# Expert slots of a decoder step: token rows turned two slots ahead and written back in place

## What is computed

```python
combine = jnp.einsum('nk,nke->ne', w_top, jax.nn.one_hot(eid, N_EXPERTS, dtype=jnp.float32)).astype(h.dtype)
out = jnp.zeros_like(hf)
for e in range(N_EXPERTS):
    act = jax.nn.silu(hf @ P['moe_w_gate'][l, e]) * (hf @ P['moe_w_up'][l, e])
    out = out + combine[:, e:e + 1] * (act @ P['moe_w_down'][l, e])
```

## Time and profile before

| What | Value |
|---|---|
| Median of three runs | 2000.77 us |
| Lowest and highest run | 1998.65 and 2010.49 us |
| Span of the profiled execution, first to last instruction | 1993.9 us |
| TensorE busy | 1815.5 us, 91% |
| VectorE, ScalarE busy | 34%, 26% |
| Mean granted clock of TensorE | 0.970 |
| Expert stage of layer 0, first up product's end to last | about 787 to 1058 us |
| Expert stage of layer 1 | about 1672 to 1944 us |

### The profile page before, as it was taken

How to read it: one execution, slowest core, us unless ns; L and a number is a source line. 1 busy time by engine, 2 the same in 40 slices (tenths; PEclk the granted TensorE clock), 3 DMA queues, 4 the chain that set the end, 5 groups by cost and what they waited for, 6 DMA issues and landing times.

```text
span 1993.9 us, 52709 instructions
## 1 busy us (share of the span) xinstructions
PE 1815.5 (91%) x23279; PEld 1445.3 (72%) x23279; DVE 684.8 (34%) x1812; ACT 513.2 (26%) x1199; POOL 100.7 (5%) x155
## 2 busy tenths in 40 slices
PE   5999998999987898999998899999999989999983
PEld 3776777777776677888887754785666778888882
DVE  5241135666664332110113400416777240101105
ACT  2112223333332121111111201316777231111112
POOL 2112000000000001000001000000000001000002
PEclk9999999999999898999999999998999998999996
DMA  8665744433334497999999891642000387999964
GB/s 294 188 219 199 255 150 135 137 116 99 98 98 130 128 291 289 359 372 353 374 380 239 207 197 44 206 94 66 1 2 2 80 342 285 389 367 373 363 222 153
DMA packets 186742, 413.48 MB, mean 207 GB/s; under 512 B 53686, under 2 KB 123794, under 8 KB 178034
## 3 DMA queue, kind: packets, MB, share of 16 engines
q1 hardware_dynamic: 167746, 357.95, 54.7%
q0 software_dynamic: 11040, 39.85, 5.6%
q10 hardware_dynamic: 7760, 12.79, 1.8%
HBM read 356.84 MB, written 57.91 MB: 208 GB/s over the span
## 4 chain that ended last, share of the span: by engine, by line
PE 47%; issue 7%; ACT 3%; DVE 3%; DMA 2%; DVEq 0%; POOL 0%; ACTq 0%; SPq 0%
PE bank L1984 11%; PE bank L1979 6%; PE bank L1997 5%; PE bank L2003 3%; PE bank L1705 3%; PE bank L2816 3%; PE bank L2924 2%; PE bank L2872 2%; PE bank L2961 2%; ACT xsT L2166 2%; PE bank L1961 1%; PE bank L1972 1%; DMA rows<-y_slots,pos 1%; PE bank L2748 1%; PE bank L2893 1%
## 5 line engine op out<-in xcount | busy, mean ns | idle before, releaser
L1979 PE MATMUL bank<-wg,xsT 128*32 128x384 f32 x1056 | 121.9, 500 | 17.9 <-ACT xsT L2166 17.9
L1984 PE MATMUL bank<-wg,xsT 128*32 128x128 f32 x1056 | 123.2, 278 | 0.0
L1984 PE MATMUL bank<-wu,xsT 128*32 128x128 f32 x1056 | 119.2, 273 | 2.5 <-issue 2.5
L1979 PE MATMUL bank<-wu,xsT 128*32 128x384 f32 x1056 | 117.9, 486 | 3.3 <-issue 3.3
L1997 PE MATMUL bank<-wd,actT 128*32 128x384 f32 x1056 | 117.6, 486 | 1.6 <-ACT actT L2180 1.6
L1984 PEld LDWEIGHTS bank<-wu,xsT 128*32 128x32 f32 x1056 | 115.2, 110 | 5.2 <-issue 2.7
L2003 PE MATMUL bank<-wd,actT 128*32 128x256 f32 (+1 forms) x704 | 118.2, 326 | 0.0
L1984 PEld LDWEIGHTS bank<-wg,xsT 128*32 128x32 f32 x1056 | 116.0, 112 | 1.0
L640 PE MATMUL bank<-xm,wp 128*128 128x272 f32 x480 | 113.3, 395 | 0.0
L2376 DVE COPY ys<-bank 128x384 f32<-128x384 f32 x32 | 17.8, 558 | 265.4 <-PE bank L2003 265.4
L2368 DVE TENSOR_TENSOR act<-bank,act 128x384 f32<-128x384 f32 x32 | 17.9, 558 | 255.9 <-PE bank L1984 255.9
(11 more groups left out here) (632 smaller groups left out, 4022.9 us busy)
## 6 DMA issues: line engine op xcount, KB each, us to landing
wg<-in_moe_w_gate_dram SPq DMA_DIRECT2D x22, 2048.0 KB, 17.8
wu<-in_moe_w_up_dram SPq DMA_DIRECT2D x22, 2048.0 KB, 22.4
wd<-in_moe_w_down_dram SPq DMA_DIRECT2D x22, 2048.0 KB, 18.6
xT<-in_ada_w_dram SPq DMA_DIRECT2D x40, 1024.0 KB, 5.8
w<-in_moe_w_gate_dram SPq DMA_DIRECT2D x10, 2048.0 KB, 17.0
fT<-in_moe_w_up_dram SPq DMA_DIRECT2D x10, 2048.0 KB, 22.2
gall<-in_moe_w_down_dram SPq DMA_DIRECT2D x10, 2048.0 KB, 17.4
wp<-in_rwkv_w_rkv_dram SPq DMA_DIRECT2D x24, 512.0 KB, 4.6
```

The source lines that it names most:

```text
L1979: mm = pe.matmul(ps[32 * j:32 * j + 32, 0:GW], B.xsT[:, k, 32 * j:32 * j + 32], w[:, k, 0:GW], start=k == 0, stop=k == KT - 1)
L1984: mm = pe.matmul(ps[96:128, q * 128:(q + 1) * 128], B.xsT[:, kk, 32 * q:32 * q + 32], w[:, kk, GW:FF], start=kk == 0, stop=kk == KT - 1)
```

## The change

The tile `xsT` goes. The turned rows of a slot are written into the slot's own row buffer, `B.xs[j]`, over the rows they came from. TensorE turns the rows of slot s+2 behind the up product of slot s, where it turned those of s+1. In slot 0 it turns both slot 1 (in the old place) and slot 2 (between its gate and its down product); the last two slots turn nothing. VectorE's copy waits for both halves of the turn, since it writes over rows of either. SyncE loads token rows when the up product of the slot that used the buffer is done, where it waited for the turn. A filler tile `moe_spare` of the size of `xsT` stays in its place.

```diff
-    B.xs = [sb(st, f"xs{i}", [C, D]) for i in range(2)] + [B.hx[0:C]]
+    B.xs = [sb(st, f"xs{i}", [128, D]) for i in range(2)] + [B.hx]
+    B.xsT = [x[:, 0:KT * C].rearrange("p (k c) -> p k c", k=KT) for x in B.xs]
     B.hs = B.hx[0:NS]
     B.ys = [sb(st, f"ys{i}", [128, YW]) for i in range(3)]
-    B.xsT = sb(st, "xsT", [128, KT, C])
+    sb(st, "moe_spare", [128, KT * C])
...
         e = sp.value_load(B.slot_e[0:1, bass.ds(slot, 1)], min_val=0, max_val=E_N - 1)
-        sp.wait_ge(S("x_tr"), n * 2 + 2)
+        sp.wait_ge(S("up_mm"), n * 4 + 4)
         load_tokens(j, slot)
-        sp.wait_ge(S("up_mm"), n * 4 + 4)
         load_gate_up(sp, B, io, l, j, e)
...
-    def turn(j, n, h):
-
-        if h == 0:
-            pe.wait_ge(S(f"xs_loaded{j}"), (n if j else n - l - 1) * 16)
-        for k in range(4):
-            mm = pe.transpose(bank[6 + h][:, k * C:(k + 1) * C], B.xs[j][0:C, (4 * h + k) * 128:(4 * h + k + 1) * 128], B.ident[0:C, 0:C])
-        mm.then_inc(S("x_tr"), 1)
-
-    def gate_or_up(w, ps, done):
+    def turn(j, n):
+
+        pe.wait_ge(S(f"xs_loaded{j}"), (n if j else n - l - 1) * 16)
+        for h in range(2):
+            for k in range(4):
+                mm = pe.transpose(bank[6 + h][:, k * C:(k + 1) * C], B.xs[j][0:C, (4 * h + k) * 128:(4 * h + k + 1) * 128], B.ident[0:C, 0:C])
+            mm.then_inc(S("x_tr"), 1)
+
+    def gate_or_up(x, w, ps, done):
...
-                mm = pe.matmul(ps[32 * j:32 * j + 32, 0:GW], B.xsT[:, k, 32 * j:32 * j + 32], w[:, k, 0:GW], start=k == 0, stop=k == KT - 1)
+                mm = pe.matmul(ps[32 * j:32 * j + 32, 0:GW], x[:, k, 32 * j:32 * j + 32], w[:, k, 0:GW], start=k == 0, stop=k == KT - 1)
...
-    def slot(v, j, last):
+    def slot(v, j, left):
         n = prior_uses(regs, l, v, j)
         s = slot_count(regs, l, v, j)
-        v2, j2 = (v, (j + 1) % 3) if j else (0 if v is None else v + 1, 1)
-        gate_or_up(B.wu[j], bank[1], "up_mm")
-        if not last:
-            for h in range(2):
-                turn(j2, uses(regs, l, v2, j2), h)
+        v1, j1 = slot_after(v, j)
+        v2, j2 = slot_after(v1, j1)
+        gate_or_up(B.xsT[j], B.wu[j], bank[1], "up_mm")
+        if v is None:
+            turn(j1, uses(regs, l, v1, j1))
+        elif left > 1:
+            pe.wait_ge(S("xt_ev"), s * 2 + 4)
+            turn(j2, uses(regs, l, v2, j2))
         pe.wait_ge(S("act_ready"), s + 1)
         for c in range(3):
             mm = pe.transpose(bank[2 + c // 2][:, c % 2 * 128:c % 2 * 128 + 128], B.act[:, c, :], B.ident[:])
         mm.then_inc(S("at_mm"), 1)
-        if not last:
+        if left:
             pe.wait_ge(S("xt_ev"), s * 2 + 4)
             pe.wait_ge(S("silu_done"), s + 1)
-            pe.wait_ge(S(f"wgu_loaded{j2}"), uses(regs, l, v2, j2) * 32)
-            gate_or_up(B.wg[j2], bank[0], "gate_mm")
+            pe.wait_ge(S(f"wgu_loaded{j1}"), uses(regs, l, v1, j1) * 32)
+            gate_or_up(B.xsT[j1], B.wg[j1], bank[0], "gate_mm")
+        if v is None:
+            turn(j2, uses(regs, l, v2, j2))
         pe.wait_ge(S("at_ev"), s * 2 + 2)
         pe.wait_ge(S(f"wd_loaded{j}"), n * 16 + 16)
...
-    def keep_turned(s):
+    def keep_turned(j, s):
         act.wait_ge(S("x_tr"), s * 2 + 2)
         for k in range(4, KT):
-            ins = act.activation(B.xsT[:, k], bank[7][:, (k - 4) * C:(k - 3) * C], ACT.Identity, bias=B.shift_p[:, l, k:k + 1])
+            ins = act.activation(B.xsT[j][:, k], bank[7][:, (k - 4) * C:(k - 3) * C], ACT.Identity, bias=B.shift_p[:, l, k:k + 1])
         ins.then_inc(S("xt_ev"), 1)
...
-        if not last:
-            keep_turned(s + 1)
+        if v is None:
+            keep_turned(1, s + 1)
+        elif left > 1:
+            keep_turned((j + 2) % 3, s + 2)
         act.wait_ge(S("at_mm"), s + 1)
         act.activation(B.actT[:, 0:2].rearrange("p c t -> p (c t)"), bank[2][:, 0:256], ACT.Copy).then_inc(S("at_ev"), 1)
-        if not last:
+        if left:
             silu(s + 1)
+        if v is None:
+            keep_turned(2, s + 2)
         act.wait_ge(S("downb_mm"), s * 4 + 4)
...
-    slot(None, 0, False)
+    slot(None, 0, 3)
     for j in (1, 2, 0):
-        slot(0, j, False)
+        slot(0, j, 3)
     with eng.bass.Fori(1, regs[l], engines=bass.OrderedEngineSet([eng.engine]), hint_back_edge=True) as v:
         for j in (1, 2, 0):
-            slot(v, j, False)
+            slot(v, j, 3)
     for j in (1, 2, 0):
-        slot(regs[l], j, j == 0)
+        slot(regs[l], j, -j % 3)
+
+
+def slot_after(v, j):
+
+    return (v, (j + 1) % 3) if j else (0 if v is None else v + 1, 1)
...
-    def keep_turned(s):
-        dve.wait_ge(S("x_tr"), s * 2 + 1)
-        tt(B.xsT[:, 0:4], bank[6][:, 0:4 * C].rearrange("p (k c) -> p k c", k=4), B.shift_p[:, l, 0:4].unsqueeze(2).to_broadcast([128, 4, C]),
+    def keep_turned(j, s):
+        dve.wait_ge(S("x_tr"), s * 2 + 2)
+        tt(B.xsT[j][:, 0:4], bank[6][:, 0:4 * C].rearrange("p (k c) -> p k c", k=4), B.shift_p[:, l, 0:4].unsqueeze(2).to_broadcast([128, 4, C]),
            ALU.add).then_inc(S("xt_ev"), 1)
...
         dve.wait_ge(S("silu_done"), s + 1)
         dve.wait_ge(S("up_mm"), s * 4 + 4)
         acts = B.act[:].rearrange("p c t -> p (c t)")
         tt(acts, bank[1][:, 0:GW], acts, ALU.mult).then_inc(S("act_ready"), 1)
-        if not last:
-            keep_turned(s + 1)
+        if v is None:
+            keep_turned(1, s + 1)
+        elif left > 1:
+            keep_turned((j + 2) % 3, s + 2)
         dve.wait_ge(S("at_mm"), s + 1)
         dve.tensor_copy(B.actT[:, 2], bank[3][:, 0:128]).then_inc(S("at_ev"), 1)
+        if v is None:
+            keep_turned(2, s + 2)
         dve.wait_ge(S("downa_mm"), s * 4 + 4)
         if not isinstance(n, int) or n > 0:
```

More of the change, by code:

```diff
@@ L1983, in gate_or_up @@
                 q, kk = m // KT, m % KT
-                mm = pe.matmul(ps[96:128, q * 128:(q + 1) * 128], B.xsT[:, kk, 32 * q:32 * q + 32], w[:, kk, GW:FF],
+                mm = pe.matmul(ps[96:128, q * 128:(q + 1) * 128], x[:, kk, 32 * q:32 * q + 32], w[:, kk, GW:FF],
                                start=kk == 0, stop=kk == KT - 1)
@@ L2033, in pe_moe @@
     pe.wait_ge(S("wgu_loaded0"), uses(regs, l, None, 0) * 32)
-    gate_or_up(B.wg[0], bank[0], "gate_mm")
+    gate_or_up(B.xsT[0], B.wg[0], bank[0], "gate_mm")
     slots(pe, regs, l, slot)
@@ L2193, in act_moe @@
     act.wait_ge(S("x_loaded"), 96)
-    keep_turned(slot_count(regs, l, None, 0))
+    keep_turned(0, slot_count(regs, l, None, 0))
     silu(slot_count(regs, l, None, 0))
```

## The result

The changed kernel takes 2015.54 us (median of 20 runs, 2008.71 to 2027.18), the kernel before 2006.55 us (20 runs). The ratio is 1.0061, 95% interval 1.0043 to 1.0079: slower by 12 us (the two medians alone lie 9.0 us apart). I had forecast 2006 us against 2000.77, 5 us slower, within 1%. The sign and the main mechanism were right, the size was less than half.

What follows compares the result with a forecast made beforehand. Bound: TensorE (17.9 us a slot), then the load queue (19.3 to 19.6) once turns wait for tokens. Layer 0 4.4 us later, layer 1 0.4: span 1998.7, plus 6.9 gives 2005.6, rounded to 2006 us; range 1987 to 2023.

Steps and rivals of the forecast that it cites:

- The removed wait: Gate product in each expert slot: no longer waits for the turn, saving 0.76 us, so 17.88 us a slot becomes 17.1.
- The token load: SyncE's queue: rows issued one slot before use land too late, so TensorE stalls some 2.2 to 2.5 us a slot.
- the sum of layer 0: Expert stage of layer 0: the queue leads from slot 8's tokens on; P(15) at 1062.5 against 1058.07, 4.4 us later.
- The stall of 2.5 us in up(13) lies beside that wait: Layer 0, up product of slot 13: the stall ends with the wait for slot 15's tokens, both at 1028.5 us.
- the bounds: Queue's pace from slot 8 on: 18.7 us a slot gives 1995 us in all, 20.0 us a slot gives 2012.
- The clock rival: TensorE in stalled slots: each wait drops the clock, costing 3.4 us of work; 21 us more, 2027 us; chance 0.10.
- One of my own signs of being wrong: TensorE in the expert slots: the forecast is wrong if the granted clock falls below 1.00 there.
- tokens arrive in time: Rival, turns in the expert slots: no turn waits for a load, 22.1 us less, 1979 us; chance 0.04.
- the queue runs faster when locked to TensorE: Rival, SyncE's load queue: it keeps its faster pace everywhere, 1995 us; chance 0.13.
- the gap stays: Rival, gate product: TensorE waits for VectorE instead, only in slots before the queue sets the pace; 2006 to 2008 us; chance 0.03.

Runs made afterwards that it cites:

- the second profile: The changed kernel as it is, profiled and timed once more; ratio to the kernel before 1.0076.
- 6 spare matmuls: The changed kernel with 6 extra 128x128 matmuls on TensorE ahead of the turn in slots 1 to 12; ratio to the kernel before 1.0024.
- half loads: Both kernels, loading only the first half of each down weight from slot 3 on: 2040.95 us for the kernel before, 2018.99 us for the changed one.

## Why the prediction was right in kind and short in size

**The removed wait** was right: the idle behind ScalarE is gone and a slot takes 17.0 to 17.1 us where nothing else waits (forecast 17.1). P(0) to P(1) is 18.8 us, not 17.8: slot 0's second turn costs its 0.9 us in full, since in slot 0 the gate still waits for ScalarE.

**The token load** was right in layer 0. I forecast slot 8's rows at 103.7 us behind P(0) (891.2 - 787.45) and slot 15's at 241.0. Measured were 877.22 + 17.4 - 790.10 = 104.5, and 1013.07 + 18.4 - 790.10 = 241.4; in the second profile 239.4. The issue and the time to landing of slot 8's:

```profile
877.22 0.34 SPq L1875 DMA_DIRECT2D hx<-x_slots  x1
...
hx<-x_slots SPq DMA_DIRECT2D x1, 384.0 KB, 17.4
```

From P(6) on TensorE ran at the queue's pace, 19.8 us (forecast 19.6). That is layer 0. In layer 1 TensorE took 18.3 us a slot from P(6) to P(12), and the rows landed 18.8 us apart, not 19.3: slot 15's came 234.1 us behind P(0), 3.1 earlier than I forecast (237.2). In each layer five turns waited, 1.7 us on average; I had said 14 or so in all, of 2 to 3 us. The experiments show that this is the cause: with the rows on another queue, or with less in the queue, the gain of the early turn comes out whole up to P(12) (206.1 us against 214.3), and the late wait without the early turn costs nothing.

**The step that failed** is in the sum of layer 0: "The stall of 2.5 us in up(13) lies beside that wait". I took its size from the trace of before, and put the fall of the clock at nothing in the sum. With the change the stall is 4.8 and 4.2 us in layer 0 and 4.4 in layer 1 (I had 3.3), and half clock follows it. P(12) to P(13) is 25.2 us (17.0 + 4.8 + 3.4), where I had 19.6, and TensorE reaches the turn of slot 15 at 1038.1 us, 6.6 us after its rows have landed. The queue's lead had ended. Of the 7 us or so that P(15) comes later than forecast, P(12) has 1.3, the longer stall 2.3 and the half clock 3.4. P(15) moved by 11.4 and 11.7 us in the two profiles, not 4.4; in layer 1 by 2.0 and 5.0, not 0.4. Together 13.4 and 16.7 us against the 12 us of the ratio. Layer 1 came out near the forecast by an offset: the same slot 13 cost 1.1 us more of stall and 3.4 of half clock, and the rows of slot 14, which led it, landed 2.7 us earlier than I had reckoned. (In the bounds, the slower end of layer 1 should read 1948.1, not 1947.7, which moves nothing.)

**The clock rival** had the mechanism right and its weight wrong. One of my own signs of being wrong came up with it: the granted clock did fall below 1.00 inside the slots. I had given the rival a chance of 0.10. My row against it, a stall of 3.3 us in a window of clock 1.00, was one case, and pauses of 2.1 to 2.8 us did bring the lower level. In slots 7 to 11 this cost next to nothing, since TensorE would have waited for rows anyway; in slot 13, with no wait behind it to hide in, it cost 3.4 us and, in the second profile, 6.5. The rival had 3.4 us of that kind in slot 14, and 21 us in all. The Trainium skill, TensorE: Matmul & The Clock Gate, "HAM oscillation", describes a clock that falls in each wait for a DMA; the trace after has it behind three of the five waits for rows in layer 0 and one of the five in layer 1.

**The other rivals.** That tokens arrive in time was wrong here, and is what the version on ScalarE's queue makes true: 17 us of the 22 came. That the queue runs faster when locked to TensorE was wrong in layer 0 (19.5 us a slot from slot 8 on, 19.6 before) and partly true in layer 1 (18.8, against 19.3), where it hid a part of what slot 13 cost. That the gap stays was wrong.

**What the stall is**, the instruction packets show. From P(7) to P(12), while the hardware loop repeats, the trace has no DMA packet of the kind instruction. The first one, of 16 KB (on q8 in the DMA view), starts in the slot behind the loop, and in each of the 23 stages of this study that have the stall, of 26, TensorE goes on 2.2 to 2.8 us after that start. What varies is when the packet starts: in the changed kernel 1.6 to 2.1 us after TensorE has run out of instructions, in the kernel before 0.0 and 0.7 us after, with 6 spare matmuls 1.3 us ahead of it. So the stall reads as the fetch of the code behind the loop, and its length as how late that fetch starts; no run changed the fetch itself.

Open: why it starts later with the change. A part is that TensorE gets there 0.9 us sooner: with the rows on ScalarE's queue it runs out 13.5 us behind P(12) and the packet starts at 14.2, against 14.4 and 14.4 in the kernel before. The load on the DMA engines can't be all of it, for with full loads and 6 spare matmuls the stall is 1.5 us in layer 0 and absent in layer 1. Open too is what makes a load land later that has rows behind it.

## What to carry to other kernels

A load that is asked for later or used earlier has to be held against its time to landing in the latest slot, not in the first or at the median: a queue that is slower than its user hides behind the buffers until one load is asked for only one slot ahead. A small load that is needed soon doesn't belong behind large ones that aren't; here moving it to the queue that had only the output stores turned a change that lost 12 us into one that wins 17. And a stall that is as long as the wait beside it isn't free: it can grow once the path is shorter, and the lower clock behind it comes on top.

## What the runs showed of the hardware

- TensorE's clock fell to its lower level behind pauses of 1.9 to 4.9 us within a stretch that was otherwise busy, and once behind one of 1.5 and one of 0.7 us close together. It stayed at 1.00 over stalls of 2.5 and 3.3 us in the kernel before and of 3.6 us in layer 0 with the rows between gate and up. The length of a pause alone doesn't say whether it falls.
- The order of loads in one DMA queue changed the pace for the same bytes. From slot 8 on the rows landed 19.3 to 20.0 us apart in layer 0 and 18.8 to 20.0 in layer 1 with the rows behind the down load, 19.2 and 19.3 with them between gate and up, and 18.0 to 18.7 with them behind the up load. Between the kernels of one order the pace differs by as much as 1.2 us, so a single profile doesn't measure the effect.
- A 384 KB load behind a backlog of 2 MB loads in one queue landed 15 to 30 us after its issue from slot 8 on, before and after the change; on the other queue, with the same DMA engines busy, it took 7.8 to 12.5 us.
- Behind the hardware loop TensorE stood still for 1.5 to 4.9 us in 23 of 26 stages, until 2.2 to 2.8 us after the first 16 KB instruction packet had started. The other three, two with spare matmuls and one with half loads, had no such stall.
